# Two condition tiles at a time ahead of the scores of the first attention, in a two-block transformer kernel on one Trainium2 core

## The chip, the core and the metric

The kernel runs on one core of a Trainium2 chip. Five engines work side by side and meet at semaphores: TensorE (PE, matrix products, out of SBUF into PSUM), VectorE (DVE), ScalarE (ACT), GpSimd (POOL) and SyncE (SP), which here issues most of the DMAs. Each engine takes its instructions strictly in the order in which the program wrote them, so an instruction that waits holds up all behind it. The metric is the device time of one execution in microseconds (us), as a median of runs; lower is better.

## What is computed

Two transformer blocks on 256 rows of 1024 numbers. What matters here is the first block, whose six modulation vectors come from a condition `c`:

```python
c_act = silu(c)
mod = c_act @ w_ada + b_ada              # 1024 -> 6 x 1024
sh1, sc1, g1, sh2, sc2, g2 = split(mod, 6)
h = rmsnorm(x, gain0) * (1 + sc1) + sh1
y = token_mixer(h)                       # 16 heads of 64, then @ w_out
x = x + g1 * rmsnorm(y, gain1)
h = rmsnorm(x, gain2) * (1 + sc2) + sh2
y = square(relu(h @ w1 + b1)) @ w2 + b2
x = x + g2 * rmsnorm(y, gain3)
```

The token mixer projects `h` to queries, keys and values, takes softmax(q k + bias) v per head (causal; the last eight heads with a window of 128 and a sink) and multiplies by `w_out`. The second block follows and is not touched by the change.

## The kernel before, in words

**Weights.** Each matrix is read in units of 128x1024 f32 (512 KB). To keep f32 precision, ScalarE rounds a unit to `wh` (`round_unit`, L608) and VectorE takes the rest, `wl` = raw - `wh` (`low_unit`, L966); TensorE then makes three products, hi x hi, hi x lo and lo x hi.

**The condition's product.** `c @ w_ada` is not done by TensorE alone. One tile of `w_ada` (128x1024) is multiplied on VectorE by a column of `c` and added to `ada_sum` in one instruction (`ada(i)`, L1059; I call it a condition tile). There are 40 in this scheme: 16 at the start (sh1, sc1), and 24 (g1, sh2, sc2) spread over the projection and the attention. Each waits for its tile's DMA and, from the second on, for the tile before it to have been written (`dve.wait_ge(ada_used, i)`), as both add to the same sums.

**The stream.** Until the first feed-forward begins, SyncE loads weight units and condition tiles through one ring of six slots in the order `first_stream()` writes: behind weight unit u stand `ada_after(u)` condition tiles. The item at place p is issued when the item at p - 6 has been used. Units 0 to 17 are the input projection, 18 to 25 are `w_out`. Behind unit 19 stand the eight DMAs that bring the bias of heads 8 to 15 (`dbias`).

**The attention loop.** It has 18 slots, i = 0 to 17, and each engine runs its own copy. In slot i:

- TensorE: scores of head i (`score`, L1571 and L1572); in slots 0 to 3 what is left of the input projection (`PROJ_SLOTS`); from slot 5 on one half of a product with `w_out` (`out1_half`, six matmuls, L1413 to L1415); the transposes of head i-1's probabilities (L1381), which wait for the scaled probabilities (`p_scaled`) and for ScalarE's copy of head i-2 (`pt_copied`); in odd slots from 3 on the value products of heads i-3 and i-2 (L1607, L1609).
- VectorE: bias, negation and row minimum of head i (`score_head`, L1098 and L1100); one condition tile if any is left (`ada_left`), from slot 1 on; the reciprocal of the row sums (L1126), which waits for head i's exponentials; the low part of the weight unit of that slot (`SPLIT_SLOTS`: unit 15 and 16 in slot 0, 17 in slot 1, 18 in slot 2, then one in every even slot); in odd slots from 3 on the split of an attention output into two parts (`split`, L974 and L975).
- ScalarE: the rounding of that slot's weight unit; the exponentials of head i (`exp_head`, L734); their scaling by the reciprocal (`scale_head`, L741 and L742); the copy of head i-1's transposed probabilities (`copy_probsT`, L750).

Behind slot 15's split VectorE multiplies the finished g1 sums by a gain (L1142), for which TensorE waits at L1507.

Of the kernel before, what the change touches and what calls it, by code (L numbers as in the profile page):

```python
# [85 lines left out]

def ada_after(u):

    return {5: 1, 6: 1, 7: 1, 8: 1, 9: 1, 10: 1, 11: 1, 12: 1, 13: 1, 14: 1, 15: 1, 16: 1, 17: 1, 18: 2, 19: 2, 20: 2, 21: 2, 22: 2, 23: 1}.get(u, 0)


def ada_units_after(u):
    first = ADA_FIRST + sum(ada_after(v) for v in range(u))
    return list(range(first, first + ada_after(u)))


def first_stream():

    order = [("ada", i) for i in range(ADA_FIRST)]
    i = ADA_FIRST  # L100
    for u in range(U_UP1):
        order.append(("w", u))
        order += [("ada", i + j) for j in range(ada_after(u))]
        i += ada_after(u)
    assert i == ADA_UNITS
    return order
# [2 lines left out]
BIAS_AFTER = [5, 19]  # L109
GAIN_AFTER = 23  # L110
GAIN_SLOT = 15

STREAM = first_stream()
PLACE = {item: place for place, item in enumerate(STREAM)}
# [63 lines left out]
def build_program(nc, a):  # L178
# [25 lines left out]
    with ctx:  # L204
# [155 lines left out]
        def raw_slot(r):  # L360
            return raw[:, r, :] if r < RING else raw_more[:, r - RING, :]
# [591 lines left out]
        def _(dve):  # L953
# [14 lines left out]
            def low_static(u):  # L968
                if u < U_END:
                    low_unit(u + 1, raw_place(u)[0], slot_of(u))  # L970

            def split(dst, src, done):

                link(V.tensor_copy(dst[:, 0:ROWS], src))  # L974
                V.tensor_tensor(dst[:, ROWS:], src, dst[:, 0:ROWS].bitcast(f32), ALU.subtract).then_inc(done, 1)  # L975
# [75 lines left out]
            def ada(i):  # L1051

                chunk, kt = divmod(i, KT)
                place = PLACE[("ada", i)]
                dve.wait_ge(first_full[place % FIRST_RING], 16 * (place // FIRST_RING + 1))
                if i >= 1:
                    dve.wait_ge(ada_used, i)
                sums = ada_sum[:, D * chunk:D * (chunk + 1)]
                V.scalar_tensor_tensor(out=sums, in0=raw_slot(place % FIRST_RING), scalar=cT[:, kt:kt + 1], in1=sums,  # L1059
                                       op0=ALU.mult, op1=ALU.add).then_inc(ada_used, 1)  # L1060
# [25 lines left out]
            def score_head(h, bias):  # L1086

                b = h % 2
                bank = aux[b] if h < N_HEADS else (aux[0], aux[3])[b]
                first = nsink[:, h - N_MOBA:h - N_MOBA + 1] if N_MOBA <= h < N_HEADS else big[:, 0:1]  # L1090
                if h >= 2:
                    dve.wait_ge(exped, 2 * (h - 1))
                if h >= N_HEADS:
                    dve.wait_ge(w_exped, 4)
                if N_MOBA <= h < N_HEADS:
                    V.tensor_copy(logits[:, b, 128:386:257], first.to_broadcast([P, 2]))
                dve.wait_ge(scores, h + 1)
                V.tensor_tensor_reduce(out=logits[:, b, 0:128], in0=bank[:, 0:128], in1=bias[:, 128:256], scale=-1.0,  # L1098
                                       scalar=first, op0=ALU.add, op1=ALU.min, accum_out=nmax[:, h, 0:1]).then_inc(scored, 1)
                V.tensor_tensor_reduce(out=logits[:, b, 129:385], in0=bank[:, 128:384], in1=bias[:, 0:256], scale=-1.0,  # L1100
                                       scalar=first, op0=ALU.add, op1=ALU.min, accum_out=nmax[:, h, 1:2]).then_inc(scored, 1)
# [11 lines left out]
            ada_left = []  # L1113
            for i in range(N_HEADS + 2):
                if i < N_HEADS:
                    if i % N_MOBA == 0:
                        dve.wait_ge(bias_loaded[i // N_MOBA], 16 * P // COPIES)
                    score_head(i, dbias[:, i, :])
                    if i == 0:
                        low_static(U_FIRST_SLOT)  # L1120
                        ada_left += ada_units_after(U_FIRST_SLOT)
                    else:
                        if ada_left:
                            ada(ada_left.pop(0))
                    dve.wait_ge(exped, 2 * i + 2)
                    V.reciprocal(rsum[:, i, :], lsum[:, i, :]).then_inc(sums_inverted, 1)  # L1126
                for k in SPLIT_SLOTS.get(i, []):
                    if k != U_FIRST_SLOT:
                        low_static(k)
                        ada_left += ada_units_after(k)  # L1130
                if i >= 3 and i % 2 == 1:
                    p = (i - 3) // 2
                    dve.wait_ge(pv_done, 2 * p + 2)
                    if p == 0:
                        dve.wait_ge(unit_done, U_OUT1)
                    split(xT[:, p, :], aux[3][:, 0:ROWS], mix_ready)
                if i == GAIN_SLOT:
                    assert not ada_left
                    dve.wait_ge(ada_used, ADA_UNITS)
                    dve.wait_ge(gain_loaded, 16)  # L1140
                    sums = ada_sum[:, D * C_G1:D * (C_G1 + 1)]
                    V.tensor_tensor(sums, sums, G1[:, :], ALU.mult).then_inc(gain_scaled, 1)  # L1142
# [118 lines left out]
            for n in range(N_BRANCH):  # L1261
                for k in range(KT + 2):
                    i = n * (KT + 2) + k
# [113 lines left out]
        def _(pe):  # L1377
# [189 lines left out]
            def score(h):  # L1567
                q, k, _, bank, _, _ = head_operands(h)
                if h >= 2:
                    pe.wait_ge(scored, 2 * (h - 1))  # L1570
                mm(bank[:, 0:128], q[:, 0:P], k[:, 0:P], start=True, stop=True)  # L1571
                mm(bank[:, 128:384], q[:, P:ROWS], k, start=True, stop=True).then_inc(scores, 1)  # L1572

            def score_pair(h):

                pe.wait_ge(scored, 2 * h)
                heads = []
                for b in range(2):
                    q, k, _, bank, _, _ = head_operands(h + b)
                    o, f = HD * b, h + b - N_HEADS  # L1580
                    heads.append((bank, q, k, cumq[o:o + AUG, f, :], cumk[o:o + AUG, f, :]))
                for bank, q, k, cq, ck in heads:
                    mm(bank[:, 0:128], q[:, 0:P], k[:, 0:P], start=True, stop=False)
                for bank, q, k, cq, ck in heads:
                    mm(bank[:, 0:128], cq[:, 0:P], ck[:, 0:P], start=False, stop=True)
                for bank, q, k, cq, ck in heads:
                    mm(bank[:, 128:384], q[:, P:ROWS], k, start=True, stop=False)
                for bank, q, k, cq, ck in heads:
                    mm(bank[:, 128:384], cq[:, P:], ck, start=False, stop=True).then_inc(scores, 1)
# [305 lines left out]
```

## Time and profile before

| | us |
|---|---|
| median of 3 runs | 764.01 (763.96 to 764.33) |
| the profiled execution | 762.43 |
| its span on the core | 760.7 |
| TensorE busy | 724.7 (95%) |
| VectorE busy | 509.5 (67%) |
| ScalarE busy | 436.2 (57%) |

The attention loop runs from 74.6 us (VectorE's first score) to about 143 us. The page's slices show TensorE busy at 9 tenths or more from the third slice (38 us) nearly to the end; matmuls are pipelined, so such a digit says that work was in flight, and the timeline has to say whether the engine waited. The granted TensorE clock is full in all slices. The rows below are from the timelines of single engines, in which a row gives the start, the length, the engine and line, the operation with output and inputs, and in square brackets the idle time before it with what ended it. A length runs until the result is written; the next instruction may start a little earlier.

### The profile page before, as it was taken

To read this page: it belongs to the slowest core of one execution; us is meant where nothing else is said; L and a number is where in the kernel's file an instruction comes from. 1 tells how busy PE (TensorE), PEld (TensorE's weight loads), DVE (VectorE), ACT (ScalarE), POOL (GpSimd) and SP (SyncE) were. 2 spreads that over 40 slices of the span, in tenths; PEclk is the share of its full clock that TensorE was granted. 3 is DMA by queue.
4 is the path that set the end of the run, shared out by engine and by line. 5 is a ranking of instruction groups with operands and counts; after the bars stand their busy time and mean duration, and the time that the engine had idled before them with its cause. 6 is when DMAs were issued, how large, how long until landed. Compare 5 with 4: busy or idle time off the path is not lost.

```text
span 760.7 us, 12115 instructions
## 1 busy us (share of the span) xinstructions
PE 724.7 (95%) x4146; PEld 616.2 (81%) x4146; DVE 509.5 (67%) x734; ACT 436.2 (57%) x684; POOL 39.4 (5%) x69
## 2 busy tenths in 40 slices
PE   0599999999999999999999999999999999999998
PEld 0488976689999887777989787887788888888886
DVE  6788579787877744347646754856667777777443
ACT  0555768666666533345544587565556777776331
POOL 4100000100000100005102000000000000000000
PEclk9999999999999999999999999999999999999999
DMA  8999788447877765444775545555455666675651
GB/s 309 354 327 384 211 223 297 139 150 212 245 225 259 243 202 177 161 143 111 213 203 159 196 143 167 166 158 178 140 155 147 190 192 191 176 208 187 206 193 57
DMA packets 137551, 152.08 MB, mean 200 GB/s; under 512 B 6187, under 2 KB 111782, under 8 KB 137512
## 3 DMA queue, kind: packets, MB, share of 16 engines
q1 hardware_dynamic: 135710, 146.85, 61.9%
q10 hardware_dynamic: 1804, 4.74, 1.8%
q8 instruction: 23, 0.38, 0.2%
q14 instruction: 14, 0.11, 0.0%
HBM read 150.13 MB, written 1.44 MB: 199 GB/s over the span
## 4 chain that ended last, share of the span: by engine, by line
PE 51%; DVE 2%; issue 0%; ACT 0%; DVEq 0%; ACTq 0%
PE acc L1405 11%; PE acc L1413 10%; PE acc L1415 9%; PE acc L1414 9%; PE acc L1406 6%; PE acc L1394 1%; PE acc L1393 1%; PE acc L1392 1%; PE aux L1381 1%; DVE wl L966 0%; DVE x_rows L1035 0%; PE aux L1607 0%; ACT wh L608 0%; PE aux L1801 0%; DVE rows_tmp L1259 0%
## 5 line engine op out<-in xcount | busy, mean ns | idle before, releaser
L966 DVE TENSOR_TENSOR wl<-raw,wh 128x1024 fp32r<-128x1024 f32 x215 | 263.7, 1233 | 155.3 <-ACT wh L608 154.3
L608 ACT ACTIVATE wh<-raw 128x1024 fp32r<-128x1024 f32 x215 | 226.2, 1056 | 136.8 <-PE acc L1415 124.9
L1392 PE MATMUL acc<-xT,wh 128*128 128x256 f32 x440 | 125.2, 285 | 3.4 <-DVE xT L1008 2.2
L1393 PE MATMUL acc<-xT,wh 128*128 128x256 f32 x440 | 124.5, 283 | 0.0
L1394 PE MATMUL acc<-xT,wl 128*128 128x256 f32 x440 | 124.5, 283 | 0.0
L1405 PE MATMUL acc<-xT,wh 128*128 128x512 f32 x352 | 122.2, 391 | 0.3 <-DVE xT L999 0.3
L1413 PE MATMUL acc<-wh,xT 128*128 128x512 f32 (+1 forms) x272 | 108.0, 397 | 0.3 <-issue 0.3
L1414 PE MATMUL acc<-wl,xT 128*128 128x512 f32 (+1 forms) x272 | 104.3, 384 | 0.0
L1415 PE MATMUL acc<-wh,xT 128*128 128x512 f32 (+1 forms) x272 | 104.3, 383 | 0.0
L1406 PE MATMUL acc<-xT,wl 128*128 128x256 f32 x352 | 98.6, 280 | 0.0
L1392 PEld LDWEIGHTS acc<-xT,wh 128*128 128x128 f32 x440 | 84.4, 192 | 5.7 <-DVE xT L1008 2.3
L1413 PE MATMUL acc<-wh,hid 128*128 128x512 f32 x216 | 84.6, 392 | 0.0
L1393 PEld LDWEIGHTS acc<-xT,wh 128*128 128x128 f32 x440 | 84.4, 192 | 0.1
L1394 PEld LDWEIGHTS acc<-xT,wl 128*128 128x128 f32 x440 | 84.4, 192 | 0.0
L1414 PE MATMUL acc<-wl,hid 128*128 128x512 f32 x216 | 84.1, 389 | 0.0
L1415 PE MATMUL acc<-wh,hid 128*128 128x512 f32 x216 | 84.1, 389 | 0.0
L1405 PEld LDWEIGHTS acc<-xT,wh 128*128 128x128 f32 x352 | 65.8, 187 | 15.1 <-issue 0.7
L1406 PEld LDWEIGHTS acc<-xT,wl 128*128 128x128 f32 x352 | 66.5, 189 | 0.0
L1413 PEld LDWEIGHTS acc<-wh,xT 128*128 128x128 f32 x272 | 51.1, 188 | 16.1 <-issue 6.5
L1415 PEld LDWEIGHTS acc<-wh,xT 128*128 128x128 f32 x272 | 51.1, 188 | 10.4
L1414 PEld LDWEIGHTS acc<-wl,xT 128*128 128x128 f32 x272 | 51.2, 188 | 9.3 <-issue 0.5
L1413 PEld LDWEIGHTS acc<-wh,hid 128*128 128x128 f32 x216 | 40.6, 188 | 11.3 <-issue 3.0
(274 smaller groups left out, 861.3 us busy)
## 6 DMA issues: line engine op xcount, KB each, us to landing
raw<-in_w_in SPq DMA_DIRECT2D x66, 512.0 KB, 3.8
raw<-in_w SPq DMA_DIRECT2D x64, 512.0 KB, 4.1
raw<-in_w_ffn_in SPq DMA_DIRECT2D x44, 512.0 KB, 4.4
raw<-in_w_ada SPq DMA_DIRECT2D x29, 512.0 KB, 5.9
raw<-in_w_ffn_out SPq DMA_DIRECT2D x22, 512.0 KB, 4.2
raw_more<-in_w_ada SPq DMA_DIRECT2D x11, 512.0 KB, 7.4
raw<-in_w_out SPq DMA_DIRECT2D x11, 512.0 KB, 3.3
rows_tmp<-in_w_ada ACTq DMA_DIRECT2D x8, 512.0 KB
```

The source lines that it names most:

```text
L608: A(wh[:, s, :], raw_unit, ACT.Copy).then_inc(rounded, 1)
L966: V.tensor_tensor(wl[:, s, :], raw_slot(r), wh[:, s, :].bitcast(f32), ALU.subtract).then_inc(split_ready, 1)
L1381: return mm(out, in_, ident[0:n, 0:n], start=True, stop=True, is_transpose=True)
L1392: mm(bank[:, 0:ROWS], wh[:, s, w], hi, start=(kt == 0), stop=False)
L1393: mm(bank[:, 0:ROWS], wh[:, s, w], lo, start=False, stop=False)
L1394: ins = mm(bank[:, 0:ROWS], wl[:, s, w], hi, start=False, stop=(kt == KT - 1))
L1405: mm(bank[:, :], wh[:, s, w], moving[:, kt, :], start=(kt == 0), stop=False, skip_group_check=True)
L1406: ins = mm(bank[:, 0:ROWS], wl[:, s, w], moving[:, kt, 0:ROWS], start=False, stop=(kt == KT - 1), skip_group_check=True)
L1413: mm(bank, hi, wh[:, s, cols], start=first, stop=False)
L1414: mm(bank, hi, wl[:, s, cols], start=False, stop=False)
L1415: return mm(bank, lo, wh[:, s, cols], start=False, stop=last)
```

## The change

The table `ada_after` puts two condition tiles behind each of the weight units 15 to 21 and none behind 22 and 23; before, it was one behind 15 to 17, two behind 18 to 22 and one behind 23. A new table says in which slots VectorE takes condition tiles: two in each of 1, 2, 3, 4, 5, 7 and 9. They now stand at the top of the slot, ahead of the head's scores; before, one stood behind the scores in each of the slots 1 to 14. The ten tiles ahead of the loop are as before, and so is all work of TensorE and ScalarE.

```diff
-    return {5: 1, 6: 1, 7: 1, 8: 1, 9: 1, 10: 1, 11: 1, 12: 1, 13: 1, 14: 1, 15: 1, 16: 1, 17: 1, 18: 2, 19: 2, 20: 2, 21: 2, 22: 2, 23: 1}.get(u, 0)
+    return {5: 1, 6: 1, 7: 1, 8: 1, 9: 1, 10: 1, 11: 1, 12: 1, 13: 1, 14: 1, 15: 2, 16: 2, 17: 2, 18: 2, 19: 2, 20: 2, 21: 2}.get(u, 0)
...
+ADA_SLOTS = {1: 2, 2: 2, 3: 2, 4: 2, 5: 2, 7: 2, 9: 2}
...
             for i in range(N_HEADS + 2):
                 if i < N_HEADS:
+                    for _ in range(ADA_SLOTS.get(i, 0)):
+                        ada(ada_left.pop(0))
                     if i % N_MOBA == 0:
                         dve.wait_ge(bias_loaded[i // N_MOBA], 16 * P // COPIES)
                     score_head(i, dbias[:, i, :])
                     if i == 0:
                         low_static(U_FIRST_SLOT)
                         ada_left += ada_units_after(U_FIRST_SLOT)
-                    else:
-                        if ada_left:
-                            ada(ada_left.pop(0))
                     dve.wait_ge(exped, 2 * i + 2)
```

VectorE's order from the split of slot 3 to the low part of slot 4, before (`xT<-aux` is the split, `logits,nmax<-aux` the score of head 4, `ada_sum` a condition tile, `rsum` the reciprocal, `wl` the low part of unit 19; the row behind each score is the read of its minimum):

```order
L974 CAST xT<-aux 128x256
L975 TENSOR_TENSOR xT<-aux,xT 128x256
L1098 ISA logits,nmax<-aux,dbias,big 128x128
L1098 ISA nmax 128x1
L1100 ISA logits,nmax<-aux,dbias,big 128x256
L1100 ISA nmax 128x1
L1059 SCALAR_TENSOR_TENSOR ada_sum<-raw,cT,ada_sum 128x1024
L1126 RECIPROCAL rsum<-lsum 128x2
L966 TENSOR_TENSOR wl<-raw,wh 128x1024
```

and the same place now:

```order
L975 CAST xT<-aux 128x256
L976 TENSOR_TENSOR xT<-aux,xT 128x256
L1060 SCALAR_TENSOR_TENSOR ada_sum<-raw,cT,ada_sum 128x1024
L1060 SCALAR_TENSOR_TENSOR ada_sum<-raw_more,cT,ada_sum 128x1024
L1099 ISA logits,nmax<-aux,dbias,big 128x128
L1099 ISA nmax 128x1
L1101 ISA logits,nmax<-aux,dbias,big 128x256
L1101 ISA nmax 128x1
L1126 RECIPROCAL rsum<-lsum 128x2
L967 TENSOR_TENSOR wl<-raw_more,wh 128x1024
L1060 SCALAR_TENSOR_TENSOR ada_sum<-raw,cT,ada_sum 128x1024 x2
```

One condition tile stood between the score of head 4 and its reciprocal; now two stand between the split and the score, and none between the score and the reciprocal. Lines from L108 on have moved down by one until L1125.

VectorE's order from the low part of weight unit 22 in slot 10 to the split of slot 11, before (`logits<-nsink` puts in the sinks of the later heads):

```order
L966 TENSOR_TENSOR wl<-raw_more,wh 128x1024
L1096 COPY logits<-nsink 128x2
L1098 ISA logits,nmax<-aux,dbias,nsink 128x128
L1098 ISA nmax 128x1
L1100 ISA logits,nmax<-aux,dbias,nsink 128x256
L1100 ISA nmax 128x1
L1059 SCALAR_TENSOR_TENSOR ada_sum<-raw_more,cT,ada_sum 128x1024
L1126 RECIPROCAL rsum<-lsum 128x2
L974 CAST xT<-aux 128x256
```

and now, the same rows of the program:

```order
L967 TENSOR_TENSOR wl<-raw,wh 128x1024
L1097 COPY logits<-nsink 128x2
L1099 ISA logits,nmax<-aux,dbias,nsink 128x128
L1099 ISA nmax 128x1
L1101 ISA logits,nmax<-aux,dbias,nsink 128x256
L1101 ISA nmax 128x1
L1126 RECIPROCAL rsum<-lsum 128x2
L975 CAST xT<-aux 128x256
L976 TENSOR_TENSOR xT<-aux,xT 128x256
```

The condition tile between head 11's score and its reciprocal is gone; the same holds for slots 10, 12, 13 and 14. Unit 22 now lies in another slot of the ring.

## Rows read from the trace of the kernel before

**Rows 1.** Busy time of each engine in four stretches of 20 us; PEclk is the clock.

```profile
core 0: us, PE busy (x) PEld busy (x) DVE busy (x) ACT busy (x) POOL busy (x), PEclk, DMA share, GB/s
0.00:20.00 20.00, 1.72 (x3) 0.31 (x3) 12.27 (x11) 1.49 (x2) 7.74 (x25) 1.00 0.88 314
...
80.00:100.00 20.00, 20.00 (x159) 18.05 (x158) 8.95 (x22) 11.29 (x32) 0.00 (x0) 1.00 0.79 176
100.00:120.00 20.00, 19.37 (x104) 13.01 (x103) 19.06 (x55) 16.14 (x47) 0.00 (x0) 1.00 0.71 235
120.00:140.00 20.00, 19.79 (x106) 13.38 (x105) 18.00 (x47) 16.89 (x48) 0.00 (x0) 1.00 0.82 276
```

**Rows 2.** Timeline of VectorE, slots 1 to 3: start, length, [idle before <- releaser].

```profile
81.67 0.35 DVE L1098 CUSTOM_DVE_ANT_0 logits<-aux,dbias,big 128x128 f32<-128x128 f32 x1 [1.34 <-PE aux L1572]
...
86.02 0.35 DVE L1098 CUSTOM_DVE_ANT_0 logits<-aux,dbias,big 128x128 f32<-128x128 f32 x1 [1.20 <-PE aux L1572]
...
93.14 0.35 DVE L1098 CUSTOM_DVE_ANT_0 logits<-aux,dbias,big 128x128 f32<-128x128 f32 x1 [3.96 <-PE aux L1572]
...
99.73 0.42 DVE L974 CAST xT<-aux 128x256 fp32r<-128x256 f32 x1 [4.55 <-PE aux L1609]
```

**Rows 3.** Timeline of VectorE: four condition tiles in a row in the first stage.

```profile
26.68 5.45 DVE L1059 SCALAR_TENSOR_TENSOR ada_sum<-raw,cT,ada_sum 128x1024 f32<-128x1024 f32 x4
```

**Rows 4.** Timeline of VectorE, slots 4 and 5.

```profile
100.65 0.35 DVE L1098 CUSTOM_DVE_ANT_0 logits<-aux,dbias,big 128x128 f32<-128x128 f32 x1
...
101.33 1.28 DVE L1059 SCALAR_TENSOR_TENSOR ada_sum<-raw,cT,ada_sum 128x1024 f32<-128x1024 f32 x1
102.53 0.16 DVE L1126 RECIPROCAL rsum<-lsum 128x2 f32<-128x2 f32 x1
...
103.72 0.35 DVE L1098 CUSTOM_DVE_ANT_0 logits<-aux,dbias,big 128x128 f32<-128x128 f32 x1
...
104.40 1.28 DVE L1059 SCALAR_TENSOR_TENSOR ada_sum<-raw,cT,ada_sum 128x1024 f32<-128x1024 f32 x1
105.59 0.16 DVE L1126 RECIPROCAL rsum<-lsum 128x2 f32<-128x2 f32 x1
```

**Rows 5.** Timeline of ScalarE, last step of the exponentials, heads 4, 5, 6, 7, 9.

```profile
101.86 0.19 ACT L734 ACTIVATION_READ_ACCUMULATOR probs<-logits,nmax 128x1 f32 x1
...
104.93 0.19 ACT L734 ACTIVATION_READ_ACCUMULATOR probs<-logits,nmax 128x1 f32 x1
...
108.60 0.19 ACT L734 ACTIVATION_READ_ACCUMULATOR probs<-logits,nmax 128x1 f32 x1
...
111.24 0.18 ACT L734 ACTIVATION_READ_ACCUMULATOR probs<-logits,nmax 128x1 f32 x1
...
117.61 0.19 ACT L734 ACTIVATION_READ_ACCUMULATOR probs<-logits,nmax 128x1 f32 x1
```

**Rows 6.** Timeline of VectorE, the reciprocals of heads 6, 7 and 9.

```profile
108.82 0.17 DVE L1126 RECIPROCAL rsum<-lsum 128x2 f32<-128x2 f32 x1 [0.42 <-ACT probs L734]
...
111.90 0.16 DVE L1126 RECIPROCAL rsum<-lsum 128x2 f32<-128x2 f32 x1
...
118.27 0.16 DVE L1126 RECIPROCAL rsum<-lsum 128x2 f32<-128x2 f32 x1
```

**Rows 7.** Timeline of TensorE, slots 5, 10, 11 and 12.

```profile
104.04 0.52 PE L1381 MATMUL aux<-ident,probs 128*128 128x128 f32 x3 [0.63 <-ACT probsT L750]
...
117.98 0.48 PE L1571 MATMUL aux<-kT,qT 64*128 64x128 f32 x2
...
123.09 0.49 PE L1381 MATMUL aux<-ident,probs 128*128 128x128 f32 x3
...
124.32 0.49 PE L1571 MATMUL aux<-kT,qT 64*128 64x128 f32 x2
```

**Rows 8.** Timeline of ScalarE, the copy of head 9's transposed probabilities.

```profile
122.41 0.47 ACT L750 ACTIVATE probsT<-aux 128x384 f32<-128x384 f32 x1
```

**Rows 9.** Timeline of TensorE behind the last head.

```profile
139.24 1.98 PE L1507 MATMUL aux<-ada_sum,ones 128*128 128x512 f32 x4 [0.21 <-DVE ada_sum L1142]
```

**Rows 10.** DMA issues from 80 to 100 us: count, size, median us from issue to landing.

```profile
raw_more<-in_w_out SPq DMA_DIRECT2D x1, 512.0 KB, 8.8
```

## Prediction

> **What bounds the kernel now.** I read three views, in this order. First the busy time by stretch [rows 1]: between 80 and 100 us VectorE works 9 of 20 us, between 100 and 140 it works 37 of 40, and TensorE's work is in flight in all but 0.8 of those 40. So there are two stretches in the attention: an early one in which VectorE has time, and a late one in which two engines are both nearly full. The clock is 1.00 throughout.
>
> Second, VectorE's timeline. Up to the split of slot 3 it waits four times for TensorE, 1.34 + 1.20 + 3.96 + 4.55 = 11.05 us in sum [rows 2]; TensorE is busy with the last projection units and waits for nobody. From the split's end at 100.65 on this turns round: VectorE goes from one instruction to the next [rows 4] and waits only for the exponentials, 0.42 us in slot 6 [rows 6].
>
> Third, TensorE's timeline: it waits 0.63 us in slot 5 and then not again until 139.24, where 0.21 us are for the g1 sums [rows 7, 9]. These two waits are the 0.8 us that rows 1 lack. Its pair of slots takes 124.32 - 117.98 = 6.34 us, back to back. So from slot 6 on TensorE sets the pace, but by very little: ScalarE's copy of head 9 ends at 122.41 + 0.47 = 122.88 [rows 8], and the transposes that need it start at 123.09 [rows 7]. The slack of the chain VectorE - ScalarE against TensorE is 0.21 us at this point, of which a semaphore takes some; I take 0.1. Whatever delays the chain by more than 0.1 us between slots 4 and 10 delays TensorE, and nothing behind gives it back, as TensorE is full.
>
> **What a pair of condition tiles costs.** Four in a row take 5.45 us and the last of them counts 1.28, so the pitch with a wait on the one before is (5.45 - 1.28)/3 = 1.39 us [rows 3]. Where the next instruction doesn't wait for the tile, it starts 102.53 - 101.33 = 1.20 later [rows 4]. A pair ahead of a score is 1.39 + 1.20 = 2.59 us.
>
> The Trainium skill says otherwise about the pitch: in "VectorE: DVE Perf Modes", section "The DRAIN you can't avoid", chained operations with a semaphore behind each take no longer than without. The rows differ, 1.39 against 1.20. By the page a pair would be 2.40, and the sum below 7.7 instead of 8.5.
>
> **What a single tile behind the score costs.** It lies beside the exponentials. In slot 4 these end at 101.86 + 0.19 = 102.05 [rows 5]; a reciprocal that only waits for them follows 0.03 later (108.60 + 0.19 = 108.79, then 108.82) [rows 5, 6]. It started at 102.53, so the tile cost 102.53 - 102.08 = 0.45. In slot 5 it is 105.59 - 105.15 = 0.44 [rows 4, 5], in slot 7 111.90 - 111.45 = 0.45, in slot 9 118.27 - 117.83 = 0.44 [rows 5, 6]. In slots 6 and 8 it cost nothing, because there ScalarE rounds a weight unit first and the exponentials end after the tile (0.42 us idle in slot 6). This is what the change gives up: before, a tile was hidden for two thirds or wholly.
>
> **The change slot by slot.**
>
> - Slots 1 to 3, nothing on the path. Three pairs are 7.77 us where three single tiles were 3.6, and three waits for exponentials, which the tiles covered, come into the open (each some 0.7 us: 102.05 less 101.33, where the tile of slot 4 began). That is 4.2 + 2.1 = 6.3 us, and the idle time up to the split is 11.05 [rows 2]. The split at 99.73 waits for a value product that TensorE reaches when the projection is done. The cover is the projection; if it were 5 us shorter, the pairs would show.
> - Slot 4. The split ends at 100.65 as before. The pair moves the score by 2.59, the missing tile behind it gives back 0.45: the reciprocal is 2.14 late. Queued behind the pair are the score, ScalarE's exponentials and scaling, and TensorE's transposes of head 4.
> - Slot 5. A second pair, + 2.59 - 0.44: 4.29 late.
> - Slot 6, none, and its tile was free: no change.
> - Slot 7, + 2.59 - 0.45: 6.43. Slot 8 as slot 6.
> - Slot 9, + 2.59 - 0.44: 8.58 late.
> - Less the slack of 0.1: TensorE is 8.5 us late in slot 10.
> - Slots 10 to 14. The chain loses its tiles and gains 0.44 us in slots 11 and 13 each, 0.9 in all. TensorE's 6.34 us a pair have no tile in them, so it cannot follow; the 0.9 become slack. The gain of g1 (L1142) stands behind a split that waits for TensorE anyway, so it is late by the same 8.5.
>
> The sum is 4 x 2.59 - 1.78 - 0.1 = 8.5 us.
>
> **Moved DMAs.** SyncE loads in another order, and each item is issued when the one six places ahead is used. The place that comes nearest is slot 5: its tiles are issued when slot 3's are used, at about 92 to 94.5 us, behind the bias DMAs; the slowest landing around there was 8.8 us [rows 10], which makes 103.3. They are needed at 102.0 + 1.4 + 2.5, some 105.9 (two tiles, the exponentials, the low part of unit 19). Unit 18 now stands behind two tiles that wait for slot 1's, and may hold slot 2's exponentials by up to 1.5 us; that is within the 4.7 us that slots 1 to 3 leave. I cost both at nothing; if one fails, it adds 1 to 3 us.
>
> **The profiled execution** of before took 762.43, which gives 770.9. It lay 1.6 below the median of 764.01, so the forecast for the median is 764.01 + 8.5 = 772.5. About 0.2% (1.5 us) is what a measurement of this kernel can tell from no change.
>
> **Rivals.**
>
> - *Half of it is absorbed.* The pairs of slots 7 and 9 might fit into the times in which VectorE waits. Against it: those waits (0.42) are in the even slots, and the pairs stand ahead of the odd scores. The pairs of slots 4 and 5 alone make 4.3: 768.3. Chance 0.08.
> - *Work counts, not order; the time doesn't grow.* In slots 4 to 14 eleven tiles were taken and now eight, and three go into idle time. If the chain's length were given by VectorE's busy time (19.06 of 20 us in rows 1 speaks for it), the pairs would replace singles one for one, and what is left is the gain of slots 11 and 13: 764.0 - 0.9 = 763.1, if TensorE could take it. It decides if the score of an odd slot has idle time ahead of it. The rows of slot 5 speak against it: score at 103.72 straight behind the low part [rows 4]. Chance 0.07, a third of it on the faster side of the bound.
> - *The second tile of a pair starts as early as any other instruction.* Then a pair is 2 x 1.20 = 2.40 and the sum 4 x 2.40 - 1.78 - 0.1 = 7.7: 771.7. Against it stand the four tiles in a row at 1.39 [rows 3]; for it, that the pitch in the loop has not been seen. Chance 0.10. (The Trainium skill's sentence above is this case.)
> - *The clock falls.* TensorE would now wait up to 2.9 us at a time in slot 5 and 8.5 in all. The one stretch of the trace with an idle TensorE is the first, 1.72 of 20 us busy, and the granted clock there is 1.00, the 2.4 GHz level [rows 1]. If it fell to 1.2 GHz for slots 6 to 13, up to 25.4 us of matmuls would double, of which 8.5 fill the waits: 764.0 + 8.5 + 16.9 = 789. Chance 0.03.
> - *A transfer is late* (above): 773.5 to 775.5. Chance 0.06.
>
> The forecast itself has 0.66, with a range of its own of 771.8 to 773.5.
>
> **How the numbers follow.** Predicted is the likeliest case, 772.5. From 769.5 to 774.5 it takes in the forecast, the early second tile, half of the late transfer and a part of the first rival, and leaves out the rest; that is a little over 8 in 10. Faster by over 0.2%: 0.03. Within 0.2%: 0.04. Slower by over 0.2%: 0.93.
>
> **What would show it.** In the profile after: the score of head 4 at about 103.2 instead of 100.65; those of heads 5, 7 and 9 with two tiles straight ahead; reciprocals of heads 4, 5, 7 and 9 about 2.1, 4.3, 6.4 and 8.6 us late, all with a wait for ScalarE ahead of them; TensorE waiting at the transposes (L1381) from slot 5 to slot 11, about 8.5 us more in sum, and not from slot 12 on; the head 3 score still at 93 to 94.5. A pitch within a pair of 1.20 would make the sum 7.7. It would be wrong if TensorE's first matmul of the feed-forward were late by clearly less than 8 us, or if scores waited for DMAs.

## The result, and the profile after

| | before | changed |
|---|---|---|
| median of 5 runs, us | 764.01 (763.79 to 764.39) | 772.17 (771.46 to 773.23) |
| the profiled execution, us | 762.43 | 772.17 |
| its span on the core, us | 760.7 | 770.5 |
| TensorE's product with the g1 sums starts, us | 139.24 | 148.96 |

The kernel became slower by a factor of 1.0105 (95% interval 1.0088 to 1.0122), 8.2 us by the medians. The two profiled executions lie further apart, 9.7 us: the one of the kernel before was 1.6 us below its median, the one of the changed kernel is its median.

VectorE in slots 3 to 5 of the changed kernel, timeline (start, length, line, operation, [idle before <- releaser]); it answers to rows 4:

```profile
100.01 0.42 DVE L975 CAST xT<-aux 128x256 fp32r<-128x256 f32 x1 [2.35 <-PE aux L1609]
...
100.81 1.28 DVE L1060 SCALAR_TENSOR_TENSOR ada_sum<-raw,cT,ada_sum 128x1024 f32<-128x1024 f32 x1
102.19 1.28 DVE L1060 SCALAR_TENSOR_TENSOR ada_sum<-raw_more,cT,ada_sum 128x1024 f32<-128x1024 f32 x1
103.39 0.34 DVE L1099 CUSTOM_DVE_ANT_0 logits<-aux,dbias,big 128x128 f32<-128x128 f32 x1
...
104.81 0.17 DVE L1126 RECIPROCAL rsum<-lsum 128x2 f32<-128x2 f32 x1 [0.67 <-ACT probs L735]
...
106.02 2.67 DVE L1060 SCALAR_TENSOR_TENSOR ada_sum<-raw,cT,ada_sum 128x1024 f32<-128x1024 f32 x2
108.60 0.34 DVE L1099 CUSTOM_DVE_ANT_0 logits<-aux,dbias,big 128x128 f32<-128x128 f32 x1
...
110.03 0.17 DVE L1126 RECIPROCAL rsum<-lsum 128x2 f32<-128x2 f32 x1 [0.67 <-ACT probs L735]
```

The split starts at 100.01, where it started at 99.73 before [rows 2], and the pair begins 0.16 us later than head 4's score did before (100.81 against 100.65). Two tiles stand at a pitch of 102.19 - 100.81 = 1.38 us, then the score at 103.39, and the reciprocal at 104.81, 2.28 us later than in rows 4, of which 0.16 were there already. Each reciprocal now waits 0.67 us for ScalarE: this is the time that a tile used to fill. Head 5's is 110.03 - 105.59 = 4.44 late.

TensorE in slots 5 to 12 and behind the last head, timeline; it answers to rows 7 and 9:

```profile
106.33 0.88 PE L1381 MATMUL aux<-ident,probs 128*128 128x128 f32 x3 [2.63 <-ACT probsT L751]
...
120.00 0.52 PE L1381 MATMUL aux<-ident,probs 128*128 128x128 f32 x3 [0.69 <-ACT probsT L751]
...
123.23 0.52 PE L1381 MATMUL aux<-ident,probs 128*128 128x128 f32 x3 [0.28 <-ACT probsT L751]
...
128.51 0.52 PE L1381 MATMUL aux<-ident,probs 128*128 128x128 f32 x3 [1.52 <-ACT probsT L751]
128.96 0.49 PE L1571 MATMUL aux<-kT,qT 64*128 64x128 f32 x2
...
134.07 0.49 PE L1571 MATMUL aux<-kT,qT 64*128 64x128 f32 x2
```

```profile
148.96 1.98 PE L1507 MATMUL aux<-ada_sum,ones 128*128 128x512 f32 x4 [0.23 <-DVE ada_sum L1142]
```

Before, TensorE waited at these transposes (L1381) once, 0.63 us. Now it waits 2.63, 0.69, 0.28 and 1.52 us by these rows, 5.12 in sum. The last two rows of the first fence tell something else: from the scores of head 11 (128.96) to those of head 12 (134.07) it takes 5.11 us without a wait. In rows 7 a whole pair of slots takes 6.34. The stretches say why; PEclk is the granted clock, 1.00 the 2.4 GHz level, 0.50 the 1.2 GHz level:

```profile
core 0: us, PE busy (x) PEld busy (x) DVE busy (x) ACT busy (x) POOL busy (x), PEclk, DMA share, GB/s
104.00:106.00 2.00, 0.00 (x0) 0.00 (x0) 1.33 (x4) 1.77 (x7) 0.00 (x0) 0.96 0.91 346
106.00:108.00 2.00, 1.67 (x7) 1.04 (x9) 1.90 (x3) 0.19 (x1) 0.00 (x0) 0.50 0.75 238
110.00:112.00 2.00, 2.00 (x5) 1.49 (x5) 1.58 (x7) 1.77 (x4) 0.00 (x0) 0.50 0.90 322
126.00:128.00 2.00, 0.99 (x5) 0.46 (x3) 1.29 (x7) 1.77 (x7) 0.00 (x0) 1.00 0.83 226
129.00:129.50 0.50, 0.50 (x4) 0.47 (x4) 0.00 (x0) 0.50 (x2) 0.00 (x0) 1.00 0.15 4
129.50:130.00 0.50, 0.50 (x3) 0.19 (x2) 0.00 (x0) 0.50 (x3) 0.00 (x0) 0.74 0.00 0
130.00:132.00 2.00, 2.00 (x5) 1.61 (x6) 1.78 (x6) 1.48 (x6) 0.00 (x0) 0.50 0.00 0
132.00:134.00 2.00, 2.00 (x13) 1.16 (x12) 0.42 (x3) 1.69 (x6) 0.00 (x0) 0.71 0.39 104
```

In both places TensorE's clock fell to the lower level and came back. The first fall began at the end of the wait of slot 5 (the first row has 0.96 and no matmul in it), the second a microsecond after the wait of slot 10, which ended at 128.51 (1.00 up to 129.5, then 0.74). In the kernel before it was 1.00 in every stretch of the attention.

### The profile page after: what moved, and what is told of

Its sections match the earlier page's. It is cut to its first block, busy times and chain, and to the rows that moved or that the text cites. A ratio compares the mean times of both kernels' runs of the same rounds, so it can differ in the third digit from the quotient of the medians.

```text
span 770.5 us, 12115 instructions
## 1 busy us (share of the span) xinstructions
PE 729.9 (95%) x4146; PEld 619.5 (80%) x4146; DVE 510.6 (66%) x734; ACT 436.9 (57%) x684; POOL 39.5 (5%) x69
## 4 chain that ended last, share of the span: by engine, by line
PE 51%; DVE 2%; issue 0%; ACT 0%; DVEq 0%; ACTq 0%
PE acc L1405 10%; PE acc L1413 9%; PE acc L1415 9%; PE acc L1414 9%; PE acc L1406 5%; PE acc L1394 1%; PE acc L1392 1%; PE acc L1393 1%; PE aux L1381 1%; DVE wl L967 0%; DVE x_rows L1036 0%; PE aux L1607 0%; ACT wh L609 0%; PE aux L1801 0%; DVE rows_tmp L1259 0%
## 5 line engine op out<-in xcount | busy, mean ns | idle before, releaser
L1405 PE MATMUL acc<-xT,wh 128*128 128x512 f32 x352 | 122.2, 391 | 0.3 <-DVE xT L1000 0.3
L1405 PEld LDWEIGHTS acc<-xT,wh 128*128 128x128 f32 x352 | 65.8, 187 | 15.0 <-issue 0.7
```

The costliest lines, as they stand in the source:

```text
L1405: mm(bank[:, :], wh[:, s, w], moving[:, kt, :], start=(kt == 0), stop=False, skip_group_check=True)
```

## Experiments

Each kernel is timed against the kernel before on the same chip. Two things outside the attention differ from one execution to the next, and move a time by a microsecond or two (last section). The kernel before scatters too: its executions beside e9 run from 761.5 to 767.3 us. So beside the ratio I give a number of the profile that holds only the attention: the time from TensorE's scores of head 4 (the start of slot 4, which nothing in slots 1 to 3 moved) to its product with the g1 sums. For the kernel before it starts here, and ends with the row of rows 9:

```profile
99.58 0.48 PE L1571 MATMUL aux<-kT,qT 64*128 64x128 f32 x2
```

| kernel | head 4's scores | g1 product | stretch, us | ratio to before (95%) |
|---|---|---|---|---|
| before | 99.58 | 139.24 | 39.7 | |
| changed | 99.86 | 148.96 | 49.1 | 1.0105 (1.0088 to 1.0122) |
| e5, changed again | 100.40 | 149.48 | 49.1 | 1.0110 (1.0079 to 1.0141) |
| e1, pairs in slots 1 to 3 only | 100.79 | 140.41 | 39.6 | 1.0028 (1.0011 to 1.0046) |
| e9, e1 again | 100.16 | 140.11 | 40.0 | 1.0002 (0.9980 to 1.0023) |
| e2, pairs behind the scores | 99.29 | 144.41 | 45.1 | 1.0083 (1.0054 to 1.0112) |
| e3, singles ahead of the scores | 99.39 | 144.97 | 45.6 | 1.0079 (1.0053 to 1.0105) |
| e4, before with short tiles from slot 4 on | 98.87 | 138.00 | 39.1 | 1.0005 (0.9987 to 1.0024) |
| e6, changed, scores repeated | 99.14 | 147.16 | 48.0 | 1.0119 (1.0085 to 1.0153) |
| e7, changed, short tiles from slot 4 on | 100.55 | 140.13 | 39.6 | 1.0012 (0.9994 to 1.0030) |
| e8, early pairs and singles | 100.11 | 139.25 | 39.1 | 0.9987 (0.9973 to 1.0001) |
| e10, e8 again | 101.02 | 140.22 | 39.2 | 0.9976 (0.9957 to 0.9994) |

### e1 and e9: the early pairs alone

```diff
-ADA_SLOTS = {1: 2, 2: 2, 3: 2, 4: 2, 5: 2, 7: 2, 9: 2}
+ADA_SLOTS = {1: 2, 2: 2, 3: 2}
...
                         ada_left += ada_units_after(U_FIRST_SLOT)
+                    elif i > 3 and ada_left:
+                        ada(ada_left.pop(0))
```

Expected: 

> The changed kernel with its pairs in slots 1 to 3 only; the other eight tiles are taken singly behind the scores in slots 4 to 11, as in the kernel before. My theory (the pairs of slots 4, 5, 7 and 9, ahead of the scores, are the whole loss): 764.0, within 0.5 us of the kernel before; head 4's score at 100.7 to 100.9 us. Rival (the early pairs and the new order of loads cost too): 766 or more. If some of the gain of tiles that leave slots 12 to 14 reached TensorE: 763.1.

Measured: the stretch is that of the kernel before, 39.6 us, but the median was 2.4 us above it, more than I had allowed. Its profile showed 1.5 us lost between 41 us and head 4. TensorE's clock had fallen twice ahead of the attention (0.66 in the stretch from 30 to 35 us and 0.66 from 40 to 45), and the second fall lies in that part. So I ran it again.

> The kernel of e1 once more (pairs in slots 1 to 3, singles behind the scores in slots 4 to 11). Its profile showed the attention as long as before (39.6 us), yet its median lay 2.4 us above. If that was the draw of the executions (TensorE's clock falls in some of them between 30 and 45 us, ahead of the attention, in the kernel before as well), the median now lies within 1 us of the kernel before. If the early pairs with unit 18 loaded late cost time in most executions, it is again 2 us or more above, and the profile shows where.

Measured the second time: median 763.63 against 764.56 before, the ratio within its interval at 1. The surplus of the first time did not come back. In the stretch, the pairs of slots 1 to 3 cost nothing beyond 0.3 us (39.6 and 40.0 against 39.7); the medians alone, 2.4 above and 0.9 below, would not settle it. In the changed kernel's profile, 9.4 of the 9.7 us lie behind head 4's scores.

### e7: what is left when the late pairs are short

```diff
-            def ada(i):
+            def ada(i, width=D):
...
-                sums = ada_sum[:, D * chunk:D * (chunk + 1)]
+                sums = ada_sum[:, D * chunk:D * chunk + width]
...
                     for _ in range(ADA_SLOTS.get(i, 0)):
-                        ada(ada_left.pop(0))
+                        ada(ada_left.pop(0), D if i < 4 else 8)
```

The tile's input is cut to the same width; the sums of the other 1016 columns are left out.

Expected: 

> The changed kernel, with the condition tiles of slots 4, 5, 7 and 9 cut from 1024 to 8 columns (the rest of their sums is left out), places and waits kept. Theory (the time of those four pairs is the whole loss, and the low clock comes from the waits that they make): the stretch from head 4's scores to the g1 product is back at 39.5 us or below, give or take 0.5, with the clock at 1.00. Rival (their waits or the changed order of loads cost by themselves): above 41.

Measured: 39.6 us. The places, the waits and the order of loads are those of the changed kernel; only the length of eight instructions is gone (0.22 us each instead of 1.28), and with it the whole 9.4 us and the low clock in the attention (this profile has one low stretch, between 40 and 45 us). The cause is the time of these pairs.

### e4: who sets the pace from slot 6 on

The same cut made to the kernel before, from slot 4 on (eleven tiles, again with their sums left out):

```diff
                     else:
                         if ada_left:
-                            ada(ada_left.pop(0))
+                            ada(ada_left.pop(0), D if i < 4 else 8)
```

Expected: 

> The kernel before, with the condition tiles of slots 4 to 14 cut from 1024 to 8 columns (the rest of their sums is left out), all waits kept. My theory (TensorE sets the pace from slot 6 on, at 6.34 us a pair of slots): VectorE gets 11 tiles' time free and the kernel gains next to nothing, 763.5 to 764.0. Rival (the chain of VectorE and ScalarE sets the pace): slots 5, 7, 9, 11, 13 and 4 give 0.44 each, 761.4.

Measured: a stretch of 39.1, 0.5 us shorter, for eleven tiles taken off VectorE. TensorE's pace is the bound in the kernel before, and it is the reason that the tiles taken out of slots 10 to 14 brought nothing. The 0.5 us are nearly all one wait, at the transposes of slot 5, 0.19 us here where rows 7 have 0.63:

```profile
98.87 0.48 PE L1571 MATMUL aux<-kT,qT 64*128 64x128 f32 x2
...
102.89 0.52 PE L1381 MATMUL aux<-ident,probs 128*128 128x128 f32 x3 [0.19 <-ACT probsT L750]
...
138.00 1.98 PE L1507 MATMUL aux<-ada_sum,ones 128*128 128x512 f32 x4 [0.21 <-DVE ada_sum L1142]
```

### e2 and e3: place and number, each alone

e2 has the pairs of the changed kernel, taken behind the scores:

```diff
                 if i < N_HEADS:
-                    for _ in range(ADA_SLOTS.get(i, 0)):
-                        ada(ada_left.pop(0))
...
                         ada_left += ada_units_after(U_FIRST_SLOT)
+                    for _ in range(ADA_SLOTS.get(i, 0)):
+                        ada(ada_left.pop(0))
```

Expected: 

> The changed kernel with the same pairs in the same slots, but behind the scores instead of ahead of them. My theory (place and size both count): a pair behind a score costs 2.59 less the 0.75 of the exponentials that it covers, which is 1.39 us more than the single tile that stood there; four such slots are 5.6, and 5.5 past the slack: 769.5, and about a microsecond more if TensorE's clock falls in a wait. Rival (only the number of tiles per slot counts): 772.2, as the changed kernel. Rival (only the place ahead of the score counts): 764.

e3 is the kernel before, with its single tiles moved ahead of the scores:

```diff
                 if i < N_HEADS:
+                    if i >= 1 and ada_left:
+                        ada(ada_left.pop(0))
                     if i % N_MOBA == 0:
...
-                    else:
-                        if ada_left:
-                            ada(ada_left.pop(0))
```

Expected: 

> The kernel before, with its single tiles in slots 1 to 14 moved ahead of the scores. My theory: in slots 4, 5, 7, 9, 11 and 13 a tile then costs 1.20 us instead of 0.45, 0.75 more each, 4.5 in sum; in slots 6, 8, 10, 12 and 14, where ScalarE rounds a weight unit first, some 0.2 each, 1 in sum; 5.5 us, so 769.5. Rival (a single tile still fits into TensorE's pace; only pairs hurt): 764 to 765.

Measured: e2's stretch is 45.1, 5.5 more than before, the very 4 x 1.39 - 0.1; e3's is 45.6, 5.9 more, where I had worked out 5.5. Neither number nor place explains the loss alone: a pair behind a score still has 0.75 us of it covered by the exponentials, a single ahead of a score has nothing. TensorE's clock stayed at 1.00 in the attention of both. In e3 head 4's score starts 0.88 us later than in rows 4, and its reciprocal follows 1.43 behind it, with a wait, as in the changed kernel:

```profile
101.53 0.35 DVE L1098 CUSTOM_DVE_ANT_0 logits<-aux,dbias,big 128x128 f32<-128x128 f32 x1
...
102.96 0.17 DVE L1125 RECIPROCAL rsum<-lsum 128x2 f32<-128x2 f32 x1 [0.67 <-ACT probs L734]
```

By the medians e2 and e3 lie 7.2 and 7.6 us above the kernel before, more than the stretches. e2's profiled execution is 5.2 us above that of the kernel before, and e3's has 2.3 us outside the attention (last section); that the rest is scatter of the medians isn't shown run by run.

### e5 and e6: the clock

e5 is the changed kernel once more.

Expected: 

> The changed kernel as it is, once more, to see whether the fall of TensorE's clock in its waits repeats. In the first profile it took 49.1 us from TensorE's scores of head 4 to its product with the g1 sums (39.7 in the kernel before), of which some 1.1 us lie in a stretch of half clock behind the wait of slot 10. If the falls belong to the waits, they come again at slots 5 to 6 and near slot 10; the time is 8 to 10 us above the kernel before in the same call.

Measured: 771.88 against 763.02, 8.9 us; the stretch 49.08, and the clock low again between 106 and 113 and between 130 and 133 us.

e6 keeps TensorE at work where it waits:

```diff
-                mm(bank[:, 0:128], q[:, 0:P], k[:, 0:P], start=True, stop=True)
-                mm(bank[:, 128:384], q[:, P:ROWS], k, start=True, stop=True).then_inc(scores, 1)
+                for again in range(3 if h in (5, 6, 8, 10) else 1):
+                    mm(bank[:, 0:128], q[:, 0:P], k[:, 0:P], start=True, stop=True)
+                    ins = mm(bank[:, 128:384], q[:, P:ROWS], k, start=True, stop=True)
+                ins.then_inc(scores, 1)
```

Expected: 

> The changed kernel, with TensorE computing the scores of heads 5, 6, 8 and 10 three times over (the same result; 1.7 us of matmuls more in each of these slots, where it waits at least 1.5 us). Theory (the chain of VectorE and ScalarE makes TensorE wait, and the low clock behind the waits costs a microsecond): the granted clock stays at 1.00 in the attention, and the stretch from head 4's scores to the g1 product takes 48.1 us, 1 less than in the changed kernel, though TensorE does 6.8 us more. Rival (TensorE's own work is the bound there): 6.8 us longer, 55.9. Rival (the low clock costs nothing): 49.1.

Measured: the repeated scores are less than I had worked out. Head 5's take 102.62 - 100.47 = 2.15 us up to the next product, where the changed kernel takes 102.04 - 101.19 = 0.85, so 1.3 more in each of the four slots and 5.2 in sum, not 6.8 (both from TensorE's timelines). With them the stretch is 1.08 us shorter, 48.0, and not 5 us longer. The clock is full throughout the attention. Slot 11 takes 132.28 - 128.24 = 4.04 with a wait of 0.28 in it, instead of 5.11 without one; in the kernel before, where head 11's scores start at 120.75, it takes 124.32 - 120.75 = 3.57:

```profile
core 0: us, PE busy (x) PEld busy (x) DVE busy (x) ACT busy (x) POOL busy (x), PEclk, DMA share, GB/s
105.00:110.00 5.00, 4.39 (x27) 3.35 (x28) 4.19 (x10) 1.97 (x8) 0.00 (x0) 1.00 0.87 274
110.00:115.00 5.00, 4.57 (x25) 2.73 (x25) 3.39 (x8) 3.68 (x10) 0.00 (x0) 1.00 0.37 132
125.00:130.00 5.00, 4.78 (x23) 3.21 (x22) 2.75 (x14) 4.30 (x13) 0.00 (x0) 1.00 0.59 124
130.00:135.00 5.00, 4.72 (x28) 3.02 (x26) 3.29 (x14) 4.48 (x14) 0.00 (x0) 1.00 0.36 105
```

```profile
99.14 0.48 PE L1572 MATMUL aux<-kT,qT 64*128 64x128 f32 x2
...
105.61 0.52 PE L1381 MATMUL aux<-ident,probs 128*128 128x128 f32 x3 [1.32 <-ACT probsT L751]
...
127.80 0.52 PE L1381 MATMUL aux<-ident,probs 128*128 128x128 f32 x3 [0.22 <-ACT probsT L751]
128.24 0.48 PE L1572 MATMUL aux<-kT,qT 64*128 64x128 f32 x2
...
131.03 0.52 PE L1381 MATMUL aux<-ident,probs 128*128 128x128 f32 x3 [0.28 <-ACT probsT L751]
...
132.28 0.48 PE L1572 MATMUL aux<-kT,qT 64*128 64x128 f32 x2
...
147.16 1.98 PE L1507 MATMUL aux<-ada_sum,ones 128*128 128x512 f32 x4 [0.21 <-DVE ada_sum L1142]
```

So the 9.4 us of the profile are two things: 48.02 - 39.66 = 8.36 us in which the chain of VectorE and ScalarE holds TensorE up, and 49.10 - 48.02 = 1.08 us of low clock. Only the second fall costs. The transposes of slot 10 start 128.51 - 99.86 = 28.65 us behind head 4's scores in the changed kernel and 127.80 - 99.14 = 28.66 in e6, so up to there the first fall had cost nothing: TensorE's slow matmuls lay within a time in which it would have waited. From there to the scores of head 12 it is 5.56 against 4.48. As a change to the kernel, repeating scores is of no use; the ratio (1.0119) doesn't show the microsecond, since its interval is wider than that.

### e8 and e10: a version with what was learned

Pairs ahead of the scores in slots 1 to 3 only, none in 4 and 5, singles behind the scores from slot 6 to 13, and unit 18 loaded ahead of slot 3's tiles:

```diff
-    ... 15: 2, 16: 2, 17: 2, 18: 2, 19: 2, 20: 2, 21: 2}
+    ... 15: 2, 16: 2, 17: 0, 18: 2, 19: 1, 20: 2, 21: 2, 22: 2, 23: 1}
...
-ADA_SLOTS = {1: 2, 2: 2, 3: 2, 4: 2, 5: 2, 7: 2, 9: 2}
+ADA_SLOTS = {1: 2, 2: 2, 3: 2}
...
+                    elif i >= 6 and ada_left:
+                        ada(ada_left.pop(0))
```

Expected: 

> A version that takes what the early stretch offers: pairs ahead of the scores in slots 1 to 3 only, no tile in slots 4 and 5, one tile behind the score in each of slots 6 to 13, and unit 18 loaded ahead of slot 3's tiles. Theory (TensorE sets the pace from slot 6 on; it waits 0.63 us in slot 5 for a chain that the tile of slot 4 lengthens by 0.45): the stretch from head 4's scores to the g1 product takes 39.2 us instead of 39.7, the kernel 0.4 us less than before, which can hardly be told; the reciprocal of head 2 at 89 to 90 us instead of 92.3. Rival (early pairs hold back the projection): 1 us or more slower.

And the second time: 

> The kernel of e8 once more, to narrow its interval. Theory: 0.5 us (0.07%) less than the kernel before, the stretch from head 4's scores to the g1 product 39.1 us. If e9 is 2 us slower again and this is not, the load order of unit 18 is what costs.

Measured: stretches of 39.1 and 39.2, 0.5 us less than before, as TensorE waits 0.19 us in slot 5 and not 0.63:

```profile
100.11 0.48 PE L1573 MATMUL aux<-kT,qT 64*128 64x128 f32 x2
...
104.14 0.52 PE L1383 MATMUL aux<-ident,probs 128*128 128x128 f32 x3 [0.19 <-ACT probsT L751]
...
139.25 1.98 PE L1509 MATMUL aux<-ada_sum,ones 128*128 128x512 f32 x4 [0.21 <-DVE ada_sum L1144]
```

By time it is 0.9987 and 0.9976 of the kernel before, the second interval just below 1. The stretch supports 0.07%; that it is faster by 0.1 to 0.2% I would not claim. It has the lowest ratios of the kernels here, and shows how little the tiles have left to give: what is left of the attention is TensorE's own work.

## Why the prediction was right

The forecast was 772.5 us, the median 772.17. Point by point:

- **The bound.** TensorE sets the pace by little, and a chain that is late by more than the slack makes it late: right (e4, e7).
- **The price of a pair.** 1.39 + 1.20 = 2.59 us. The profile has 103.39 - 100.81 = 2.58 for it, 1.38 up to the second tile and 1.20 from there to the score, so the rival of 7.7 us falls. The Trainium skill ("VectorE: DVE Perf Modes", "The DRAIN you can't avoid") found for eight copies in a chain that a semaphore behind each costs nothing extra. For these tiles the trace doesn't agree: where the next instruction waits for the tile it is 1.38, where it doesn't 1.20 (that next one is another operation, and no run here has two tiles without the wait).
- **What a tile behind the score costs,** 0.45 or nothing: right. With 0.16 us taken off that the changed profile was late with already, the reciprocals of heads 4, 5, 7 and 9 are 2.12, 4.28, 6.41 and 8.56 us late, and 2.14, 4.29, 6.43 and 8.58 had been worked out. Those of heads 7 and 9, to be held against rows 6:

```profile
118.47 0.17 DVE L1126 RECIPROCAL rsum<-lsum 128x2 f32<-128x2 f32 x1 [0.67 <-ACT probs L735]
...
122.91 2.67 DVE L1060 SCALAR_TENSOR_TENSOR ada_sum<-raw,cT,ada_sum 128x1024 f32<-128x1024 f32 x2
...
126.99 0.17 DVE L1126 RECIPROCAL rsum<-lsum 128x2 f32<-128x2 f32 x1 [0.67 <-ACT probs L735]
```

- **The slack,** taken at 0.1 us: right. Counted from head 4's scores on TensorE, head 9's reciprocal stands at 126.99 - 99.86 = 27.13 in the changed kernel and at 118.27 - 99.58 = 18.69 before, 8.44 later, and the chain alone made the stretch 8.36 longer (e6): 0.08 us.
- **Slots 1 to 3,** nothing: right in the result, mis-sized on the way. Unit 18, behind two tiles in the ring, came 6.6 us after its issue at 83.68 and held head 2's exponentials: 3.10 us of wait before the reciprocal, 2.4 more than the 0.67 at the others, where I had allowed 1.5. Head 3's score came at 96.06, not at 93 to 94.5 as foretold. The split's own wait shrank from 4.55 to 2.35 us but did not vanish, so this stayed covered. First ScalarE and its wait for that load, then VectorE:

```profile
90.30 1.06 ACT L609 ACTIVATE wh<-raw 128x1024 fp32r<-128x1024 f32 x1 [4.03 <-DMA raw<-in_w_out]
```

```profile
92.27 0.17 DVE L1126 RECIPROCAL rsum<-lsum 128x2 f32<-128x2 f32 x1 [3.10 <-ACT probs L735]
...
96.06 0.35 DVE L1099 CUSTOM_DVE_ANT_0 logits<-aux,dbias,big 128x128 f32<-128x128 f32 x1
```

With unit 18 loaded ahead of the tiles (e8) that wait is gone, though the reciprocal comes at 91.0 and not at 89 to 90:

```profile
90.98 0.17 DVE L1128 RECIPROCAL rsum<-lsum 128x2 f32<-128x2 f32 x1 [0.67 <-ACT probs L735]
```

- **The clock.** This step was wrong. I gave a fall a chance of 0.03 and a price of 17 us, because in the first stretch of rows 1 TensorE was nearly idle at a granted clock of 1.00. It fell twice in both profiles of the changed kernel, and its price was 1.1 us (e6): the falls lasted about 7 and 3 us instead of the whole attention, and the first lay in a time of waiting. The reading of rows 1 failed too: the clock's column says 1.00 from the start of the trace on, but the matmuls between 25.7 and 28.9 us do not bear it out. These are the 128x128 matmuls of L1381 in the kernel before, in the first long burst and then a few microseconds later, and in the changed kernel in a stretch with 0.50:

```profile
L1381 PE MATMUL aux<-ident,rows_tmp x16: 421/421/475, 25.7 to 28.9; 128*128 128x128 f32 x16
L1381 PE MATMUL acc<-ident,ada_sum x16: 272/273/421, 29.2 to 33.0; 128*128 128x128 f32 x16
```

```profile
L1381 PE MATMUL aux<-ident,probs x3: 421/421/448, 106.3 to 106.8; 128*128 128x128 f32 x3
```

These are the shortest, median and longest of one matmul in ns. The first burst stands behind an idle time of 5.11 us and has the 421 ns of the lower level, not the 273 of the full one. Judged by these lengths, the trace of the kernel before already held a low clock behind an idle TensorE, where the column has 1.00, and a chance of 0.03 was too small. The sign "about 8.5 us more" of waiting at the transposes failed with it: it was 5.12 - 0.63 = 4.5 more, as slow matmuls filled a part.

- **The level.** The profiled change is 8.36 + 1.08 + 0.28 (head 4's scores start that much later), 9.7 us; the medians say 8.2 and 8.9. The forecast of 8.5 had no clock in it, so part of its closeness is luck. Nor is the low clock the same in every execution: the profiled ones, with both falls, have a mean clock of 0.993 over the span, and of the nine timed ones four have 0.993, one 0.989, two 0.996 and two 0.998. The two with 0.998 took 771.66 and 771.10 us, but two with 0.993 took 771.46 and 771.33, so the clock alone doesn't sort the times, and what the medians lack against the profiles I can't name run by run.

The rivals: half absorbed (the reciprocals of heads 7 and 9 are late by the full price of their pairs), work instead of order (e3: the same number of tiles per slot, 5.9 us more), late transfers (one came late and stayed covered) all fell.

## What to carry to other kernels

An idle time on an engine belongs to the place where it stands. VectorE had 11 us of it up to slot 3 and nearly none after, and a rule for all slots ("ahead of the scores") was free in the first and cost its full length in the second. Ahead of the score, once the idle time is gone, a tile cost its whole 1.20 us; behind it, beside the exponentials that have to be awaited anyway, a single one cost 0.45 or nothing. So ask of each filler, before its number is counted: which wait does it lie in, and is that wait still there in this slot.

## What the runs showed of the hardware that I had not expected

**The clock falls in waits of this size.** In the changed kernel it went to the lower level at the end of a wait of 2.63 us and again about 1 us behind one of 1.52, in both profiles; in e2 it stayed full with waits up to 2.02 us, in e6 with waits up to 1.32. So the longest wait alone doesn't say whether it falls. That the waits bring the falls rests on e6 and e7, one profile each, in which the long waits are filled or gone and the clock of the attention is full. The Trainium skill ("TensorE: Matmul & The Clock Gate", "Why this matters for your kernels") says that an idle gap between matmul bursts brings the lower clock back and advises to avoid it. These runs agree in kind, with the falls at the waits of 2.63 and 1.52 us.

**It also falls ahead of the attention, by the execution.** Of the profiled executions of e1, e4, e6, e7, e8, e9 and e10, each has a stretch of low clock somewhere between 30 and 45 us (0.66 to 0.78 at the lowest, in stretches of 5 us), where TensorE waits for the first projection's inputs; those of the kernel before, of e2, of e3 and of the changed kernel have none. Other executions of the kernel before have mean clocks down to 0.995, so it has such falls too; where they lie isn't shown.

**The last feed-forward has two speeds at full clock.** From the g1 product to the end of the span most profiles take 621.5 us, but e3, e7 and e10 take 623.8 or 623.9. The difference is in the last loop. Two profiles, matmuls of L1405 (the same code; it is L1404 in e3) in 100 us of that loop, number, busy time and mean ns of one:

```profile
L1405 PE MATMUL acc<-xT,wh 128*128 128x512 f32 x290 | 100.6, 391 | 0.0
```

```profile
L1404 PE MATMUL acc<-xT,wh 128*128 128x512 f32 x284 | 100.4, 399 | 0.0
```

391 against 399 ns, and 290 against 284 of them, 2% of the loop. Nothing in it was changed, and I don't know what sets it. For a difference below 0.3% this means that one profile or one median of a few runs of this kernel is not enough, and that a stretch of the trace is the better measure.
